# A gate table kept and drained in halves of 64 tokens, with a third buffer for early weights and the down weights' high part one block ahead

## The reference, cut to what matters

```python
def peer(xn, w_q, sub_keys, u, v):
    q = (xt @ w_q).reshape(t, PEER_HEADS, 2, PEER_HALF)
    sc = jnp.einsum("thpc,hpnc->thpn", q, sub_keys).astype(jnp.float32)
    top_s, top_i = lax.top_k(sc, PEER_TOPK)
    cand_s = (top_s[:, :, 0, :, None] + top_s[:, :, 1, None, :]).reshape(t, PEER_HEADS, PEER_TOPK * PEER_TOPK)
    cand_i = (top_i[:, :, 0, :, None] * PEER_NKEYS + top_i[:, :, 1, None, :]).reshape(t, PEER_HEADS, PEER_TOPK * PEER_TOPK)
    best_s, best_pos = lax.top_k(cand_s, PEER_TOPK)
    idx = jnp.take_along_axis(cand_i, best_pos, axis=-1)
    gate = jax.nn.softmax(best_s, axis=-1)
    ...
        act = jnp.einsum("cd,ced->ce", xc, u[ic]).astype(jnp.float32)
        hid = (jax.nn.gelu(act, approximate=False) * gc).astype(xc.dtype)
        return jnp.einsum("ce,ced->cd", hid, v[ic])
```

## Time and profile before

| | |
|---|---|
| three timed runs | 2558.01, 2560.43, 2563.36 us |
| their median | 2560.43 us |
| the profiled execution, its own time | 2556.22 us |
| its span | 2554.1 us |
| mean granted TensorE clock | 0.959 of full speed |
| TensorE busy with matmuls | 2349.6 us, 92% of the span |
| VectorE, ScalarE, GpSimd busy | 55%, 29%, 15% |
| the table phase | from 601 to 1133 us of the span |
| the expert phase | from 1133 to about 1943 us |

### The profile page before, as it was taken

How to read it: one execution, slowest core, us unless ns; L and a number is a source line. 1 busy time by engine, 2 the same in 40 slices (tenths; PEclk the granted TensorE clock), 3 DMA queues, 4 the chain that set the end, 5 groups by cost and what they waited for, 6 DMA issues and landing times. The chain is left out here.

```text
span 2554.1 us, 27010 instructions
## 1 busy us (share of the span) xinstructions
PE 2349.6 (92%) x10337; PEld 1779.7 (70%) x10337; DVE 1413.6 (55%) x2545; ACT 739.7 (29%) x1301; POOL 386.3 (15%) x306
## 2 busy tenths in 40 slices
PE   7989899899988988858999999999995999989889
PEld 4457666686555656646888899999994898875444
DVE  1335423426988978528777666666666623434321
ACT  1134412321013425523333333333334332211110
POOL 1100000000243131014111122222320000013100
PEclk9999999999999999978999999999997999989899
DMA  4231132202786594579999777777771422120110
GB/s 182 95 95 34 58 123 108 83 34 74 259 276 235 184 328 138 168 248 381 328 314 318 263 263 277 264 266 275 270 277 58 146 86 99 66 108 33 50 66 33
DMA packets 174703, 444.48 MB, mean 174 GB/s; under 512 B 14704, under 2 KB 97392, under 8 KB 167792
## 3 DMA queue, kind: packets, MB, share of 16 engines
q1 hardware_dynamic: 137712, 308.53, 35.4%
q0 software_dynamic: 36864, 134.23, 14.2%
HBM read 401.22 MB, written 41.48 MB: 173 GB/s over the span
## 5 line engine op out<-in xcount | busy, mean ns | idle before, releaser
L758 PE MATMUL bank<-XT,ur 128*128 128x384 f32 x1072 | 371.7, 501 | 51.6 <-DMA ur<-in_u 51.6
L758 PEld LDWEIGHTS bank<-XT,ur 128*128 128x128 f32 x1072 | 205.0, 197 | 192.8 <-DMA ur<-in_u 63.4
L1355 PE MATMUL bank<-Vh,Hh 128*128 128x512 f32 x768 | 299.8, 390 | 7.1 <-DVE Hl L1423 7.1
L1357 PE MATMUL bank<-Vh,Hl 128*128 128x512 f32 x768 | 300.4, 391 | 0.0
L1356 PE MATMUL bank<-Vl,Hh 128*128 128x512 f32 x768 | 300.3, 391 | 0.0
L1421 DVE TENSOR_TENSOR Vl<-Vr,Vh 128x1024 fp32r<-128x1024 f32 x128 | 156.7, 1225 | 135.6 <-ACT Vh L1387 135.5
L793 POOL DMA_INDIRECT ring<-in_v,gidx x128 | 160.6, 1255 | 450.6 <-DVE acc L805 206.8
L1387 ACT ACTIVATE Vh<-Vr 128x1024 fp32r<-128x1024 f32 x128 | 135.0, 1055 | 159.2 <-PE bank L1357 144.8
L1336 PE MATMUL bank<-Xh,Uh 128*128 128x384 f32 x488 | 166.3, 341 | 13.1 <-DVE Xl L1404 7.9
L1355 PEld LDWEIGHTS bank<-Vh,Hh 128*128 128x128 f32 x768 | 144.6, 188 | 37.1 <-DVE Hl L1423 8.2
L1338 PE MATMUL bank<-Xh,Ul 128*128 128x384 f32 x488 | 165.9, 340 | 0.0
(11 more groups left out here) (314 smaller groups left out, 4350.0 us busy)
## 6 DMA issues: line engine op xcount, KB each, us to landing
ur<-in_u SPq DMA_DIRECT2D x128, 512.0 KB, 4.0
Vr<-in_v SPq DMA_DIRECT2D x128, 512.0 KB, 5.1
W<-in_w_stream SPq DMA_DIRECT2D x26, 2048.0 KB, 7.8
gates<-stage SPq DMA_DIRECT2D x48, 512.0 KB, 6.8
Gr<-gates SPq DMA_DIRECT2D x128, 192.0 KB, 5.0
w_raw<-in_w_mixer SPq DMA_DIRECT2D x14, 1024.0 KB, 4.9
early<-ar SPq DMA_DIRECT2D x67, 192.0 KB, 4.5
A<-early SPq DMA_DIRECT2D x67, 192.0 KB, 4.1
```

The source lines that it names most:

```text
L758: mm = pe.matmul(c.bank[bank + r][:, 0:DN], c.ur[:, r, k * P:(k + 1) * P], c.XT[:, k, 0:DN], start=k == 0, stop=k == KT - 1)
L1355: pe.matmul(ps, Hh[r][:, tok], Vh[r][:, cut], start=p == 0, stop=False)
L1357: mm = pe.matmul(ps, Hl[r][:, tok], Vh[r][:, cut], start=False, stop=p == PK - 1)
```

## The change

- `stage` holds two halves of 64 tokens, and each half is written out (8 pieces of 512 KB) while the next half is made. Half 0 goes out in the second part of the first tile's slices, and so on; half 5 goes out at the end. The wait of a tile for the one before becomes a wait of a half for the half before the last.
- The table in DRAM is laid out by half, pair of blocks, expert, block of the pair, token. A piece is still 1,024 runs of 512 bytes. The gates are read by pairs, every second block, as 128 by 6 runs of 512 bytes (before: one block, 128 runs of 1,536 bytes), into two buffers of a pair.
- The ring of fetched rows is 5 deep rather than 6; its space goes to a third buffer for early weights. Weights are loaded three blocks ahead.
- `EARLY` goes from 67 to 58: 8, 13, 13, 10 beside the choices, 12 beside the slices, none between tiles, 2 at the end. `LATE` goes from 61 to 70. `HEAD` goes from 3 to 2.
- Dots in the table phase go from 81 to 58: 13, 13 and 5 at the ends of the three dense choices, none between tiles. At the start of the expert phase there are 10 rather than 14; 60 rather than 33 are left for its loop.
- The first transposition comes four blocks after the end of `E_SCORE[1]`, the second and the third in the middle of the slices of the tile before.
- In the expert loop ScalarE makes `Vh` of block p + 1 before `Hh` of block p. `up` of block 2 is no longer ahead of the first down product.

```diff
-RG = 6
+RG = 5
...
-E_SCORE, E_SLICES, E_DRAIN, E_LAST = (9, 13, 13, 13), 4, 4, 3
-EARLY = sum(E_SCORE) + DT * E_SLICES + E_DRAIN + E_LAST
+E_SCORE, E_SLICES, E_LAST = (8, 13, 13, 10), 4, 2
+EARLY = sum(E_SCORE) + DT * E_SLICES + E_LAST
 LATE = PK - EARLY
-DOTS_LINK, DOTS_TAIL, DOTS_DRAIN, DOTS_FIRST = 9, 14, 12, 14
-DOTS_TABLE = DT * (DOTS_LINK + DOTS_TAIL) + DOTS_DRAIN
+DOTS_LINK, DOTS_TAIL = 9, (0, 13, 13, 5)
+DOTS_TABLE = DT * DOTS_LINK + sum(DOTS_TAIL)
+DOTS_FIRST = 10
+HALF = P // 2
+PIECES = 8
...
     def turn(self, sp, n):
         sp.wait_ge(self.done, n + 1)
-        self.load(sp, n + 2)
+        self.load(sp, n + 3)
...
-            turns(E0, EH0 + E_SLICES)
-            sp.wait_ge(copied, 2 * NSL)
-            for i in range(E_SCORE[3]):
-                for j in range(2 * i, min(2 * i + 2, CUTS)):
-                    store(0, j)
+            def store(half, first, last):
+                sp.wait_ge(copied, NSL * (half + 1))
+                for j in range(first, last):
+                    cut = slice(j * PK // PIECES, (j + 1) * PK // PIECES)
+                    pairs = slice(j * PK // PIECES // 2, (j + 1) * PK // PIECES // 2)
+                    src = stage[:, half % 2, cut].rearrange("p (a b) t -> p a (b t)", b=2)
+                    sp.dma_start(t["gates"][half, pairs].rearrange("a p b t -> p a (b t)"), src).then_inc(early.tabled[half % 2], 16)
+
+            def between(half, e):
+                store(half, 0, PIECES // 2)
+                early.turn(sp, e)
+                store(half, PIECES // 2, PIECES)
+                early.turn(sp, e + 1)
...
+            turns(E0, EH0 + 2)
+            between(0, EH0 + 2)
+            for i in range(PIECES):
+                store(1, i, i + 1)
                 early.turn(sp, E3 + i)
-            turns(EH1, E_SLICES)
-            sp.wait_ge(copied, 4 * NSL)
-            for i in range(E_DRAIN):
-                for j in range(i * CUTS // E_DRAIN, (i + 1) * CUTS // E_DRAIN):
-                    store(1, j)
-                early.turn(sp, ED + i)
-            turns(EH2, E_SLICES)
-            sp.wait_ge(copied, 6 * NSL)
-            for j in range(CUTS):
-                store(2, j)
+            turns(E3 + PIECES, E_SCORE[3] - PIECES + 2)
+            between(2, EH1 + 2)
+            between(3, EH2)
+            between(4, EH2 + 2)
+            store(5, 0, PIECES)
             turns(EL, E_LAST)
...
-                if tt >= 1:
-                    act.wait_ge(early.tabled, 16 * CUTS * tt)
                 for s in range(NSL):
+                    half = 2 * j // NSL
+                    if s % (NSL // 2) == 0 and half >= 2:
+                        act.wait_ge(early.tabled[half % 2], 16 * PIECES * (half // 2))
...
+                if p % 2 == 0:
+                    if p >= 4:
+                        sp.wait_ge(gated, p - 2)
+                    pair = t["gates"][:, n // 2].rearrange("h p b t -> p h (b t)")
+                    sp.dma_start(Gr[p // 2 % 2][:].rearrange("p h b t -> p h (b t)"), pair).then_inc(g_in[p // 2 % 2], 16)
...
+            def hi_v(p):
+                if p < PK:
+                    act.wait_ge(v_in[p % RV], 16 * (p // RV + 1))
+                    if p >= RV:
+                        act.wait_ge(summed, p - RV + 1)
+                    act.activation(Vh[p % RV][:], Vr[p % RV][:], ACT.Copy).then_inc(v_hi, 1)
...
-                act.wait_ge(v_in[r], 16 * (p // RV + 1))
-                if p >= RV:
-                    act.wait_ge(summed, p - RV + 1)
-                act.activation(Vh[r][:], Vr[r][:], ACT.Copy).then_inc(v_hi, 1)
+                hi_v(p + 1)
                 act.wait_ge(gated, p + 1)
                 act.activation(Hh[r][:], A[r][:], ACT.Copy).then_inc(h_hi, 1)
```

More of the change, by code:

```diff
@@ L734, in __init__, with buffers, table_done @@
         self.c = c
-        i0, i1, self.done, self.gelud, k0, k1 = signals(c.nc, ctx, "ue_in0 ue_in1 ue_done ue_gelud ue_kept0 ue_kept1")
-        self.u_in, self.kept = (i0, i1), (k0, k1)
-        self.tabled, = signals(c.nc, ctx, "ue_tabled")
+        i0, i1, i2, self.done, self.gelud, k0, k1, t0, t1 = signals(
+            c.nc, ctx, "ue_in0 ue_in1 ue_in2 ue_done ue_gelud ue_kept0 ue_kept1 ue_tabled0 ue_tabled1")
+        self.u_in, self.kept, self.tabled = (i0, i1, i2), (k0, k1), (t0, t1)
+    def buffers(self, *bufs):
+        self.bufs = bufs
+    def table_done(self, eng):
+        for half in range(2):
+            eng.wait_ge(self.tabled[half], TABLED)
     def load(self, sp, n):
         if n < EARLY:
-            sp.dma_start(self.c.ur[:, n % 2], self.c.t["u"][n].rearrange("p k e -> p (k e)")).then_inc(self.u_in[n % 2], 16)
+            sp.dma_start(self.bufs[n % 3], self.c.t["u"][n].rearrange("p k e -> p (k e)")).then_inc(self.u_in[n % 3], 16)
     def turn(self, sp, n):
         sp.wait_ge(self.done, n + 1)
-        self.load(sp, n + 2)
+        self.load(sp, n + 3)
         sp.wait_ge(self.gelud, n + 1)
@@ L960, in phase_table @@
         part = S2.bitcast(U32).rearrange("p (n s) -> p n s", s=SLOTS)
-        dest = t["gates"].rearrange("i j t -> j i t")
-        FIRST = [sum(E_SCORE[:n]) for n in range(TT + 1)]
         E0, E1, E2 = 0, E_SCORE[0], E_SCORE[0] + E_SCORE[1]
@@ L1027, in slices @@
                 for s in range(NSL):
+                    if s == NSL // 2 and tt < DT - 1:
+                        turn(tt + 2)
                     j, r = tt * NSL + s, s % 2
@@ L1212, in choose @@
                     return
-                dots(count["room"] + DOTS_TAIL - count["dot"])
+                dots(count["room"] + DOTS_TAIL[n] - count["dot"])
                 gates(n)
@@ L1237, in _ @@
             slices(1)
-            dots(DOTS_DRAIN)
             slices(2)
@@ L1268, in phase_experts @@
         Vl = [sb(f"Vl{i}", [P, D], F32R) for i in range(RV)]
-        Gr = [sb(f"Gr{i}", [P, DN]) for i in range(RV)]
+        Gr = [sb(f"Gr{i}", [P, 2 * DT, 2, HALF]) for i in range(2)]
         Hh = [sb(f"Hh{i}", [P, DN], F32R) for i in range(RV)]
@@ L1343, in _ @@
                 r = p % RV
-                if p == 0:
-                    up(1)
-                    up(2)
-                elif p + 1 >= HEAD and p + 1 < PK and late[p + 1]:
+                if p + 1 < PK and late[p + 1]:
                     up(lates[p + 1])
@@ L1406, in _ @@
             s, done = DOTS_TABLE, 0
-            for i in range(DOTS_FIRST):
-                if i == DOTS_FIRST // 2:
-                    lo_u(2)
+            for _ in range(DOTS_FIRST):
                 gat.dot(dve, s)
@@ L1423, in _ @@
                 dve.tensor_tensor(Hl[r][:], A[r][:], Hh[r][:].bitcast(F32), ALU.subtract).then_inc(h_lo, 1)
-                if late[p] and p > 0:
+                if late[p]:
                     lo_u(lates[p] + 2)
```

73 lines of the change are left out of this document (34 added, 39 removed).

## The result

The changed kernel takes 2531.31 us (median of 4 runs, 2530.53 to 2538.12); the kernel before took 2560.68 us on the same chip (median of 4 runs, 2558.01 to 2563.36). The ratio is 0.9881, with a 95% interval of 0.9865 to 0.9896: 1.2% faster. That is inside the range of the prediction, and 17 us above its number. The profiled execution took 2530.53 us, with a span of 2528.7 us, against 2556.2 and 2554.1 before.

The account below looks back on a forecast made before the run. TensorE was taken to bound the expert loop, while the table phase alternated between TensorE and DMA with VectorE. The terms sum to -46.2 us, from 2556.2 to 2510.0 us, 2514 as a median; range 2496 to 2542.

Parts of the forecast that it names:

- (a): Table phase: the first two dense choices end in 13 dots rather than 14, -5 us, bounds -2 and -8.
- (b): Third dense choice: five dots in its tail and 10 blocks rather than 13 beside it, -23 us, bounds -20 and -24.
- (c): Stretch between second and third tile's slices goes but for one slice, -43 us; two transpositions amid slices, +2 us.
- (d): End of the table phase: 14 us rather than 39, set by SyncE's last pieces, -25 us.
- (e): Table's end to first down product: four dots and one up product fewer ahead, -4.5 us, bounds 0 and -8.
- (f): After the first down product: 68 up products rather than 58, TensorE being the bound, +42.3 us.
- (g): Expert loop's early blocks: `Vh` one block ahead closes a ring through `Vr`'s load, +8 us, bounds 0 and +25.
- (h): First and second tile's slices: TensorE idles longer before them and starts below full clock, +2 us, bounds 0 and +4.
- the ring binds throughout: Rival: the ring through `Vr`'s load costs 38 us over 56 blocks rather than 8; 2530 to 2555 us, chance 20%.
- the gates' reads cost by the run: Rival: a block's 384 gate runs rather than 128 overload the queues, +80 us, about 2590 us; chance 4%.
- the halves don't keep apart: Rival: half 3's late pieces stall ScalarE and TensorE in the last tile's slices, 8 to 12 us, 2524 us; chance 8%.
- more is gained: Rival: no gathers waiting, 11 us at the table's end, no ring loss; 2492 to 2498 us, chance 8%.

Follow-up runs that it names:

- tail3_14: The changed kernel with `Vh` back in its own block, and 14 dots rather than 5 in the third choice's tail: 2517.2 us.
- fewer_first: The changed kernel with `Vh` in its own block, 64 early blocks, tails of 11, 11 and 4 dots, and 4 dots rather than 10 before the expert loop: 2467.5 us.
- vh_back: The changed kernel with `Vh` made in its own block again rather than one block ahead: 2503.1 us.
- adds_capped: The changed kernel with at most three adds in a block on VectorE: 2521.3 us.
- before_vh_ahead: The kernel before, with only `Vh` made one block ahead: 2567.7 us.
- adds_no_fetch: The changed kernel without the 128 gathers for the adds, VectorE adding what lies in the buffers: 2510.8 us.
- capped_no_fetch: The changed kernel with at most three adds in a block and no gathers for the adds: 2507.0 us.
- v_first: The changed kernel with SyncE issuing the load of `Vr` ahead of the load of up weights in late blocks: 2507.4 us.

## Why the prediction was right, and where it missed

The median of 2531.3 us lies in the range, but 1.3 us above the 2498 to 2530 that I called my case with 60%. Against the profiled execution the sum had 2510.0 us and it took 2530.5. In the order of the terms, with the borders of the rows above:

- **(a) choices one and two, -5:** first slices at 808.93 rather than 813.86, -4.9. Right.
- **(b) third choice, -23:** from first to second slices 112.2 us rather than 135.5, -23.3. Right, with the cause shown by `tail3_14`.
- **(c) drain stretch and turns, -41:** from second to third slices 53.9 rather than 96.8, and the third's slices 2 us longer: -40.8. Right.
- **(d) end of the table, -25:** 13.7 us rather than 39, -25.3. SyncE's eight pieces took 10.8 us rather than the 12.2 I had. As with (a) and (c), the borders in the traces show the size; no run took these terms apart.
- **(e) start of the experts, -4.5:** 30.5 us rather than 36.5, -6.0. `fewer_first` shows that the dots set it, by its trace.
- **(f) ten up products, +42.3:** `vh_back` has the whole loop without a ring: 1883.54 - 1069.81 = 813.7 us, against 1939.93 - 1169.47 = 770.5. That is +43.2. The size is right.
- **(g) `Vh` one block ahead, +8:** 7.4 us in the early blocks, 5.4 to 10.0 over the six kernels that have it. Right there, and nothing was reckoned for the late ones.
- **(h) clock, +2:** nearly nothing of it was seen. The slices take 52 us as before; the first 16 records of the first tile take 3.78 us in both kernels, those of the second 3.78 rather than 2.52.

These give 3.8 us less than forecast at the first down product. Behind the loop the kernel took 616.5 us rather than 614.2, 2.3 more, within what kernels that are equal there differ by. Two places named as signs did not follow from the sum itself: "near 926" for the second tile's slices leaves out the 5 us of (a), and "1041 to 1046" for the start of the experts is later than the 1039 that (a) to (d) give; 921.15 and 1038.7 were measured.

**The step that failed** is the sentence behind (f): "TensorE is the bound there, so this is exact". It is not the count nor the price of the up products; it is that nothing else was reckoned in the late blocks. I had worked out the ring of (g) for the early blocks alone, "5 us over 56 blocks", with two blocks for a round and a limit of 5.66 us for the landing. In a late block SyncE issues `load_u` first, that waits for `Ul`, and `Vr` behind it; the ring closes in one block and its limit is 4.71 us. It cost 21.9 us, and the bound of +25 for the whole term was passed (29.3). All the rows for it were at hand: the earlier trace rows have the steps, the period, and the order of `load_u` and `Vr` stands in the code. I had read the landing, 5.4 us in the median, where the queues are used 0.94, and never where they are used less. By itself the landing there would not have settled it either: between 1500 and 1800 us the kernel before has 4.5 us in the median and 5.7 at the most, so by its median the ring just holds, and it was the changed kernel that had 5.0 in its late part.

The Trainium skill (page "DMA: Bandwidth & Descriptors", section "Anatomy of one DMA — SWDGE (gpsimd) path") has about 2.0 us and the bytes at 436 GB/s for one transfer that GpSimd issues. `Vr` is issued by SyncE, which the prediction left unsaid when it carried the figure over. By it 512 KB would take 3.2 us, an estimate from that page, and neither ring would ever lag. No trace here has so short a landing of `Vr`: the least is 3.7 in the earlier trace rows, 3.4 in any kernel's early blocks (`adds_capped`), and 4.2 in the late blocks. The load of up weights, 512 KB too and issued 0.4 us ahead of `Vr`, comes nearer: 3.6 us in the median in the late part of the changed kernel, against 4.6 for `Vr` over the same stretch (1320 to 1900 us).

The rivals: that the ring binds throughout, at 20%, is nearest to what happened, and the time lies in its range (2530 to 2555), but the loss lay mostly in the other part of the loop. The early blocks, for which it was written, lost only 7.4 us, and its price of 38 was not reached. That the gates' reads cost by the run was wrong: `vh_back` keeps them, and TensorE is full. That the halves don't keep apart was wrong too: TensorE is busy 50.0 of 52 us in the third tile's slices, with no wait of over 2.1 us at their start. That more is gained did not come even without the late ring: `vh_back` takes 2503.1 us, above the 2492 to 2498 named for it.

What stays open: why the loads take longer in one kernel than in another. From issue to `Vh` they took 4.72 us on average in `before_vh_ahead`, 4.84 in `adds_no_fetch` and 5.09 in the changed kernel. The gates' reads are not the reason, and without the gathers most of the loss goes; but which of their number, their time of issue and the state of the ring itself lengthens the loads was not told apart. That the state of the ring matters is likely: `capped_no_fetch` has the same loads as `adds_no_fetch`, and only 9 of its 56 `Vh` from 1420 to 1880 us waited for their load, against 54 of 55.

## What to carry to other kernels

Where a step is moved ahead on an in-order engine, write down the ring for each kind of iteration, with every queue that it goes through and each wait that stands ahead in it. Compare the period with the ring's fixed steps and the mean time of the load, not its median: in the late blocks of these traces a mean of 4.72 us against a limit of 4.71 lost nothing, and 5.09 lost some 20 us over 53 blocks. Slack hides late landings for a while, and one burst of work can make them visible sooner. Here it was enough to swap two issues, so that the ring closed in two blocks. And where an engine idles by the profile in front of a bound that another sets, work can be moved there, but its loads go through queues that the bounding engine uses as well: here the first down product came 3.7 us later for 25 us of products moved out of the loop.

## What the runs showed of the hardware

In the six kernels whose traces give the landings of `Vr`, these took 4.2 or 4.3 us at the least between 1500 and 1800 us, 4.5 to 5.2 in the median and 5.7 to 7.6 at the most, though the share of the DMA engines was 0.76 to 0.81 in all of them. What such a difference costs depends on the ring: with a median of 5.2 `v_first` lost nothing in the late part, and with 4.6 `adds_capped` lost 12.7 us.

Without the gathers of the adds the share fell from 0.78 to 0.45, and the mean from issue to `Vh` only from 5.09 to 4.84 us.

Pieces of the table with 512-byte runs went out at 10.79 / 8 = 1.35 us each at the end of the table; in the kernel before it was 24.38 / 16 = 1.52 us.
